# Mixture-of-experts kernel on one core: results of experts 0 to 6 added to x by one-hot products in the next expert, in place of indirect DMAs that add in device memory

## The reference

```python
def moe_swiglu(h, w_router, w_gate, w_up, w_down):
    logits = (hf @ w_router).astype(jnp.float32)
    top_val, top_idx = lax.top_k(logits, TOP_K)          # TOP_K = 2 of 8
    gates = jax.nn.softmax(top_val, axis=-1)
    ...
    def run_block(args):
        tok, gate, e = args
        y = swiglu(hf[tok], w_gate[e], w_up[e], w_down[e])   # 1024 -> 3584 -> 1024
        return y * gate[:, None].astype(y.dtype)
    ...
    out = jnp.zeros((N, D), h.dtype).at[buf_tok].add(y.reshape(cap, D).astype(h.dtype))

x = x + moe_swiglu(h, ...)
return rmsnorm(x, final_norm)
```

## Time and profile before

| what | value |
|---|---|
| median of 3 runs (lowest, highest) | 1356.46 us (1355.63, 1356.54) |
| the profiled execution's own time | 1358.75 us |
| its span, first to last instruction | 1357.0 us |
| PE busy | 1314.3 us (97%) |
| PE weight loads busy | 941.6 us (69%) |
| DVE / ACT / POOL busy | 427.5 / 305.1 / 80.2 us |
| read from device memory | 438.70 MB |
| expert 0 begins on PE | about 504 us |

### The profile page before, as it was taken

One profiled execution on the slowest core, in us unless ns is written; L12 is line 12 of the kernel. 1 busy time (PEld: TensorE's weight loads), 2 busy tenths in 40 slices (PEclk: granted clock), 3 DMA queues, 4 the chain that ended last, 5 costly groups with the idle time before them and its releaser, 6 DMA issues.

```text
span 1357.0 us, 31023 instructions
## 1 busy us (share of the span) xinstructions
PE 1314.3 (97%) x13973; PEld 941.6 (69%) x13973; DVE 427.5 (32%) x719; ACT 305.1 (22%) x467; POOL 80.2 (6%) x76
## 2 busy tenths in 40 slices
PE   7999999999999999999999999999989999999985
PEld 7999999878888886665556666665546666665543
DVE  6987878965444560000000000000000000000002
ACT  5455455554444460000000000000000000000002
POOL 1511111010000000000000000000000000000000
PEclk9999999999999999999999999999999999999998
DMA  9644454357665578999999999999999999999993
GB/s 355 250 166 151 147 187 184 128 180 280 248 245 218 182 284 358 372 386 403 419 412 419 417 421 406 420 418 406 419 421 412 419 418 405 421 418 418 408 420 152
DMA packets 68425, 447.45 MB, mean 330 GB/s; under 512 B 7920, under 2 KB 10608, under 8 KB 16192
## 3 DMA queue, kind: packets, MB, share of 16 engines
q1 hardware_dynamic: 63456, 436.57, 80.1%
q0 software_dynamic: 4400, 8.30, 2.3%
q10 hardware_dynamic: 432, 0.54, 0.1%
HBM read 438.70 MB, written 6.68 MB: 328 GB/s over the span
## 4 chain that ended last, share of the span: by engine, by line
PE 89%; DMA 5%; SPq 4%; ACT 1%; DVE 1%; issue 1%; ACTq 0%; DVEq 0%
PE bank L1783 37%; PE bank L1802 14%; PE bank L444 10%; PE bank L446 10%; PE bank L445 10%; SPq L465 3%; DMA raw_late<-in_expert_units 2%; DMA w_raw<-in_expert_units 2%; PE bank L1730 2%; PE bank L1546 1%; PE bank L1528 1%; PE bank L1561 1%; PE bank L1762 1%; DMA qkT<-in_xT 1%; PE bank L1536 0%
## 5 line engine op out<-in xcount | busy, mean ns | idle before, releaser
L400 DVE TENSOR_TENSOR w_lo<-raw,w_hi 128x2048 fp32r<-128x2048 f32 x70 | 160.5, 2293 | 60.6 <-ACT w_hi L395 60.4
L395 ACT ACTIVATE w_hi<-raw 128x2048 fp32r<-128x2048 f32 x71 | 135.9, 1914 | 90.1 <-PE bank L446 84.1
L444 PE MATMUL bank<-w_hi,a_hi 128*128 128x256 f32 (+1 forms) x400 | 136.5, 341 | 1.0 <-DVE a_lo L1154 0.5
L446 PE MATMUL bank<-w_hi,a_lo 128*128 128x256 f32 (+1 forms) x400 | 133.9, 335 | 0.0
L445 PE MATMUL bank<-w_lo,a_hi 128*128 128x256 f32 (+1 forms) x400 | 133.9, 335 | 0.0
L1280 DVE TENSOR_TENSOR h<-sg,bank 128x384 f32<-128x384 f32 (+1 forms) x56 | 28.2, 504 | 301.8 <-PE bank L1802 163.1
L1286 DVE COPY hT_x<-bank 128x128 f32<-128x128 f32 x35 | 10.1, 290 | 352.3 <-ACT hT_x L842 352.3
L444 PE MATMUL bank<-a_hi,w_hi 128*128 128x256 f32 x384 | 112.4, 293 | 8.6 <-DVE w_lo L982 8.6
L446 PE MATMUL bank<-a_hi,w_lo 128*128 128x256 f32 x384 | 110.2, 287 | 0.0
L445 PE MATMUL bank<-a_lo,w_hi 128*128 128x256 f32 x384 | 110.2, 287 | 0.0
L842 ACT ACTIVATE hT_x<-bank 128x256 f32<-128x256 f32 x35 | 13.4, 383 | 420.1 <-PE bank L1730 420.1
(11 more groups left out here) (302 smaller groups left out, 1861.0 us busy)
## 6 DMA issues: line engine op xcount, KB each, us to landing
w_raw<-in_expert_units SPq DMA_DIRECT2D x86, 1024.0 KB, 28.1
raw<-in_units SPq DMA_DIRECT2D x71, 1024.0 KB, 4.9
raw<-in_expert_units SPq DMA_DIRECT2D x60, 1024.0 KB, 27.6
raw_more<-in_expert_units SPq DMA_DIRECT2D x45, 1024.0 KB, 27.4
raw_late<-in_expert_units SPq DMA_DIRECT2D x45, 1024.0 KB, 27.6
extra<-in_expert_units SPq DMA_DIRECT2D x30, 1024.0 KB, 26.9
a_raw<-in_expert_units SPq DMA_DIRECT2D x28, 1024.0 KB, 26.5
aside_raw<-in_expert_units SPq DMA_DIRECT2D x15, 1024.0 KB, 27.5
```

The costliest lines, as they stand in the source:

```text
L395: nc.scalar.activation(w_hi[:, u % SPLIT, :], where, ACT.Copy).then_inc(hi_ready, 1)
L400: nc.vector.tensor_tensor(w_lo[:, u % SPLIT, :], home(u)[0], w_hi[:, u % SPLIT, :].bitcast(F32), ALU.subtract).then_inc(lo_ready, 1)
L444: nc.tensor.matmul(bank, hi, w[0], start=start, stop=False)
L446: return nc.tensor.matmul(bank, lo, w[0], start=False, stop=stop)
```

## The change

It does four things.

1. The indirect DMAs that add `y_rows` to `sums` go for experts 0 to 6, with the read of `sums` (L620), the add of it (L1313) and six of the eight early stores of zeros. They stay only in the branch that is not taken.
2. ACT's `results` puts the scaled results of a token's slot side by side in one row of `y_rows` (64 rows of near tokens by 1024 columns, 32 rows of far ones): two instructions for bank 0 and, for a wide expert, four for bank 1, in place of one and one.
3. In expert i+1 PE makes four products of 128 tokens x 512 columns from `place` and `y_rows` (`place_results`), two for tokens 0 to 127 in block 0 and two for tokens 128 to 255 in block 1, into banks 0 and 1. DVE adds each to x (`add_results`). The first down unit waits for the four adds (`banks_free`).
4. `place` is now made for every expert: two transposes of `pick` in block 3 and ACT's copy. `pick_slots` moves from block 3 to 4, `slot_sums` and `slots_known` from block 4 to 5.

```diff
-            def scatter(i, parity, wide, total):
+            def scatter(i):
                 pool.wait_ge(y_scaled, i + 1)
...
             for i in range(1, E):
                 gather(i, i % 2, IS_WIDE[i])
-                total += 2 if IS_WIDE[i - 1] else 1
-                scatter(i - 1, (i - 1) % 2, IS_WIDE[i - 1], total)
-            pool.wait_ge(unit_used, U_MOE + LAST_IN_HN + 1)
-            pool.dma_start(hn[:, :, :], sums[0:SEQ, :].rearrange("(t p) d -> p t d", p=P)).then_inc(sums_back, 16)
-            pool.sem_inc(scatter_done, 1)
+            pool.wait_ge(x_added, 4)
+            pool.sem_inc(scatter_done, E)
...
-                    for table, at in ((hn_rows, EMPTY), (sums, 0), (sums, P), (sums, EMPTY)):
+                    for table, at in ((hn_rows, EMPTY), (sums, EMPTY)):
...
             def results(i, parity, wide):
                 act.wait_ge(unit_used, U_MOE + (i + 1) * UE)
                 act.wait_ge(spots_ready, i + 1)
-                if not isinstance(i, int) or i:
-                    act.wait_ge(scatter_done, i)
-                last = nc.scalar.activation(y_rows[:, 0:512], ps[0][:, :], ACT.Copy, scale=slot_gate[:, parity, 0:1])
+                for s in range(2):
+                    of = slice(s * NEAR, (s + 1) * NEAR)
+                    last = nc.scalar.activation(y_rows[0:NEAR, s * 512:(s + 1) * 512], ps[0][of, :], ACT.Copy,
+                                                scale=slot_gate[of, parity, 0:1])
                 if wide:
-                    last = nc.scalar.activation(y_rows[:, 512:768], ps[1][:, 0:256], ACT.Copy, scale=slot_gate[:, parity, 1:2])
+                    for s in range(4):
+                        of = slice(s * FAR, (s + 1) * FAR)
+                        last = nc.scalar.activation(y_rows[NEAR:WIDE, s * 256:(s + 1) * 256], ps[1][of, 0:256], ACT.Copy,
+                                                    scale=slot_gate[of, parity, 1:2])
...
-                    if last and (kind, b, half) == ("up", 2, 1):
-                        act.wait_ge(place_tr, 1)
+                    if isinstance(i, int) and (kind, b, half) == ("up", 3, 1):
+                        act.wait_ge(place_tr, i + 1)
                         nc.scalar.activation(place[:, :], ps[7][:, 0:SEQ], ACT.Copy).then_inc(place_ready, 1)
...
+            def add_results(i, t):
+
+                for n in range(2):
+                    dve.wait_ge(y_placed, 4 * i + 2 * t + n + 1)
+                    cols = x[:, t, n * 512:(n + 1) * 512]
+                    nc.vector.tensor_tensor(cols, cols, ps[n][:, :], ALU.add).then_inc(x_summed, 1)
...
+                    if i and (kind, b, half) == ("up", 0, 1):
+                        add_results(i - 1, 0)
+                    if i and (kind, b, half) == ("gate", 1, 1):
+                        add_results(i - 1, 1)
                     if i == E - 1:
-                        if (kind, b, half) == ("gate", 4, 0):
-                            dve.wait_ge(sums_back, 16)
-                            for t in range(TT):
-                                nc.vector.tensor_tensor(x[:, t, :], x[:, t, :], hn[:, t, :], ALU.add).then_inc(x_summed, 1)
                         return
-                    if (kind, b, half) == ("gate", 3, 0):
+                    if (kind, b, half) == ("gate", 4, 0):
                         pick_slots(i + 1, slice(i + 1, i + 2))
-                    if (kind, b, half) == ("up", 4, 0):
+                    if (kind, b, half) == ("up", 5, 0):
                         slots_known(i + 1, (i + 1) % 2, IS_WIDE[i + 1])
...
+            def banks_free(i):
+
+                if not isinstance(i, int):
+                    pe.wait_ge(y_scaled, i)
+                elif i:
+                    pe.wait_ge(x_summed, 4 * i)
+
+            def place_results(i, t):
+
+                pe.wait_ge(place_ready, i + 1)
+                pe.wait_ge(y_scaled, i + 1)
+                if t:
+                    pe.wait_ge(x_summed, 4 * i + 2)
+                slots = WIDE if IS_WIDE[i] else NEAR
+                for n in range(2):
+                    nc.tensor.matmul(ps[n][:, :], place[0:slots, t * P:(t + 1) * P], y_rows[0:slots, n * 512:(n + 1) * 512],
+                                     start=True, stop=True).then_inc(y_placed, 1)
...
                 for j, (kind, b, half) in enumerate(MOE_SEQ):
+                    if (kind, b, half) == ("up", 0, 1):
+                        place_results(i - 1, 0)
                     narrow_unit(i, j)
...
                     if b:
                         turn_hidden(i, b - 1, True)
                         after(b)
+                    elif isinstance(i, int) and i:
+                        place_results(i - 1, 0)
...
+                    if i and b == 1:
+                        place_results(i - 1, 1)
+                    if b == 3:
+                        pe.wait_ge(spots_ready, i + 1)
+                        for t in range(TT):
+                            first = 0 if i == E - 1 else NEAR
+                            turned = pick[:, t, :, :].rearrange("p a n -> p (a n)")[:, first:first + P]
+                            last = nc.tensor.transpose(ps[7][:, t * P:(t + 1) * P], turned.bitcast(F32), ident[:, :])
+                        last.then_inc(place_tr, 1)
...
-                    if i < E - 1 and b == 4:
+                    if i < E - 1 and b == 5:
```

More of the change, by code:

```diff
@@ L98 @@
     _free.append(_n)
-LAST_IN_HN = max(_n for _n in range(MAIN) if SLOT_OF[_n] == N_FIRST)
 AGAIN = 14
@@ L627, in _ @@
                     gather(i, 0, True)
-                    scatter(i, 0, True, 2 * (i - E + 1) + total)
+                    scatter(i)
                 pool.nop()
@@ L862, in expert @@
                         hidden_near(i, b - 1 if kind == "gate" else b + 1, wide)
-                    if last and (kind, b, half) == ("up", 2, 1):
-                        act.wait_ge(place_tr, 1)
+                    if isinstance(i, int) and (kind, b, half) == ("up", 3, 1):
+                        act.wait_ge(place_tr, i + 1)
                         nc.scalar.activation(place[:, :], ps[7][:, 0:SEQ], ACT.Copy).then_inc(place_ready, 1)
-                if not last:
+                if not isinstance(i, int):
+                    results_again(i)
+                elif not last:
                     results(i, parity, wide)
@@ L1239, in pick_slots @@
                     dve.wait_ge(row_sum_ready, i)
+                if isinstance(i, int) and i:
+                    dve.wait_ge(place_tr, i)
                 for t in range(TT):
@@ L1249, in slots_known @@
                 dve.wait_ge(row_sum_ready, i + 1)
-                if not isinstance(i, int) or i >= E:
+                if not isinstance(i, int):
                     dve.wait_ge(scatter_done, i)
                 elif i >= 2:
-                    dve.wait_ge(scatter_done, i - 1)
+                    dve.wait_ge(y_scaled, i - 1)
                 for part in range(2 if wide else 1):
@@ L1305, in after @@
                         slots_known(0, 0, IS_WIDE[0])
-                    if i == 0 and (kind, b, half) == ("gate", 4, 0):
+                    if i == 0 and (kind, b, half) == ("gate", 5, 0):
                         dve.wait_ge(overs_summed, 1)
                         nc.vector.tensor_scalar(over_i[:, :], ps[7][:, 0:1], 1.0, None, ALU.min).then_inc(routed, 1)
+                    if i and (kind, b, half) == ("up", 0, 1):
+                        add_results(i - 1, 0)
+                    if i and (kind, b, half) == ("gate", 1, 1):
+                        add_results(i - 1, 1)
                     if i == E - 1:
-                        if (kind, b, half) == ("gate", 4, 0):
-                            dve.wait_ge(sums_back, 16)
-                            for t in range(TT):
-                                nc.vector.tensor_tensor(x[:, t, :], x[:, t, :], hn[:, t, :], ALU.add).then_inc(x_summed, 1)
                         return
-                    if (kind, b, half) == ("gate", 3, 0):
+                    if (kind, b, half) == ("gate", 4, 0):
                         pick_slots(i + 1, slice(i + 1, i + 2))
-                    if (kind, b, half) == ("up", 4, 0):
+                    if (kind, b, half) == ("up", 5, 0):
                         slots_known(i + 1, (i + 1) % 2, IS_WIDE[i + 1])
@@ L1417, in _ @@
                 .then_inc(y_right_scaled, 1)
-            dve.wait_ge(x_summed, TT)
             for q, (n, t, bank) in enumerate(SCATTER):
@@ L1813, in begin @@
                     pe.wait_ge(hT_near_ready, i * N_EB + b + 1)
-                    if b == 0 and (not isinstance(i, int) or i):
-                        pe.wait_ge(y_scaled, i)
+                    if b == 0:
+                        banks_free(i)
                 if kind == "gate" and b == 0 and isinstance(i, int) and i == 0:
@@ L1896, in after @@
                         slot_sums(0, slice(0, 1), IS_WIDE[0])
-                    if i == 0 and b == 3:
-                        pe.wait_ge(spots_ready, 1)
```

(12 more changed lines are left out.)

26 lines of the change are left out of this document (15 added, 11 removed).

## The result

The changed kernel takes **1366.01 us** (median of 6 runs, 1365.22 to 1366.57) against 1356.35 for the kernel before (6 runs, 1355.63 to 1357.02): ratio 1.0072, 95% interval 1.0059 to 1.0085, so 9.7 us slower. The prediction was 1359.8 with a range to 1364.5. The kernel gets slower, as predicted, but the size is not as predicted: 2.4 us by the sum and 3.3 by the number, 9.7 as measured.

What follows compares the result with a forecast made beforehand. PE and the weight loads were taken to bound the kernel in turns. Adding 27.7 us to PE against 25.3 free ends 2.4 us later with PE alone pacing; scaled, 1359.8 us, range 1353.5 to 1364.5.

Steps and rivals of the forecast that it cites:

- The products, 3.75 us an expert: On PE in experts 1 to 7: four 512-column products at 3.44 us plus a 0.31 switch, 26.2 for seven.
- The transposes, 0.22 an expert: On PE: two added transposes of pick for each of experts 0 to 6, 0.11 each, 1.5 us in all.
- The loads stay ahead, and the relief is worth nothing: Weight loads land 10 to 18 us before last use; 16 us taken from the DMA engines counts as 0.
- One drain more for a narrow result: Narrow results' 64-row products, as their own tiling mode, might pay another switch at two experts, some 0.6 us over the sum.
- ACT and DVE, nothing on the path: At the results' hand-over: ACT's 3.1 us and DVE's 2.5 us an expert stay covered, so PE doesn't wait.
- rival 3: New wait at each hand-over from ACT or DVE, 0.5 to 1 us an expert: 1364 us, chance 0.15.
- Rival 2: Products cheaper by running beside neighbours, 20 to 25 us in all: 1354 us, chance 0.2.
- Rival 1: Loads still set the end, so bytes removed from the DMA show as time: some 1342 us, chance 0.12.
- What PE has free: 25.3 us: PE's waits for loads in experts 4, 5 and 7, 5.07 + 4.37 + 15.9, can absorb added work.
- On which scale: Profiled execution against the runs' median: 1361.2 or 1358.9 us; a third of the 2.3 us between taken, giving 1359.8.
- The gather ... cover 7 us: Gather for the next expert, a block later: some 11 us needed within 18.7, leaving 7 us cover, more in wide experts.
- the four rivals: The prediction's alternatives: loads set the end, cheaper products, hand-over waits, and adds in device memory staying (chance nil).

Runs made afterwards that it cites:

- e3: Changed kernel with every one-hot product of experts 0 to 6 made twice; 1391.46 us.
- e1: Changed kernel without the one-hot products and DVE's adds for experts 0 to 6, their results left out of x; 1343.04 us.
- e10: Kernel before, with pick also transposed and copied to place in experts 1 to 6, copies unused; 1357.81 us, one execution.
- e2: Changed kernel with POOL also making the former adds in device memory, with their waits, into a table nobody reads; 1365.95 us.
- e6: Changed kernel with POOL, in a wide expert, issuing the gather only after the far parts of block 5; 1361.30 us.
- e12: Kernel before, unedited, profiled a second time; 1355.69 us.
- e9: Kernel before, with only the slots' work (pick, slot sums, slot numbers, gather) a block later; 1356.20 us, one execution.

## Why the prediction was right in kind and short in size

**The products, 3.75 us an expert.** Measured 3.78 (81.01 - 77.23), and 3.44 for the four alone by e3, which leaves 0.34 for the switch where the prediction had 0.31. The nearest row, the 512-column unit, was the right one. Right.

**The transposes, 0.22 an expert.** 77.23 - 77.01 in e1 and e10. Right.

**The loads stay ahead, and the relief is worth nothing.** No wait for a landing from 600 to PE's last unit, and in the last 19 us before it the DMA engines are idle:

```profile
1330.00:1349.00 19.00, 19.00 (x172) 11.95 (x168) 1.43 (x4) 0.94 (x3) 0.00 (x0) 1.00 0.00 1
```

The last two units are made from 1345.2 on, so their loads were there 15 us or more before, at the upper end of the forecast's 10 to 18 or a little beyond; the loads into `hn` in 855:935 land 5.7 to 10.4 us after their issue, where it had "some 10 of the 26". e2 shows the 0. Right.

**One drain more for a narrow result.** The prediction took from the Trainium skill, "TensorEngine Tiling (Array Packing)", section Key Properties, that changing the tiling mode drains TensorE. By that rule the 64-row products of experts 2 and 5 would pay one switch more, about 0.3 us in each. The traces show none: expert 5 of e6, with 64-row products, is 4.00 over the 115.73 of a wide expert, and expert 1, with 96-row ones, is 4.00 over its 77.01. For the switch between 64 columns and the whole width they do show a price, the 0.34 above.

**ACT and DVE, nothing on the path.** The trace has no wait of PE for either at these places, and expert 4 is as long as expert 1. Right; rival 3 falls with it. Rival 2 falls by e3. Rival 1 falls with the changed profile, in which no wait for a landing is left; e1 shows that its 1342 was well placed as what the loads allow, 1343.04 with no product at all.

**"What PE has free: 25.3 us."** This is the step that failed. It was read from the earlier trace rows of one execution, as 5.07 + 4.37 + 15.9. In e12, the same program in another execution, it is: expert 4, 77.01 - 77.01 = 0; expert 5, 120.98 - 117.65 = 3.3; expert 7, 90.75 less what it takes without waits, 80.16 - 3.78 = 76.38, gives 14.4 (the same sum gives 15.8 for the first profile, where the prediction had 15.9). Together **17.7**. Then 27.7 - 17.7 = 10.0, and 1355.7 + 10.0 = 1365.7, where 1366.0 was measured.

Of the 7.6 us between 25.3 and 17.7, 2.6 are loads that ran slower in the profiled execution (720.13 - 717.57 for experts 1 to 7), and the other 5.0 are PE's own longer work: 1.9 each in experts 2 and 5 and 0.65 and 0.53 in experts 3 and 6. Most of it is the stalls beside the gathers, which e6 prices at 4.7 in the changed kernel, expert 0 included. That the new sum comes within 0.3 is luck in part. Against e12's lengths and 4.00 more, expert 2 of the changed kernel is 1.7 longer and experts 3 and 6 are 2.0 and 1.2 shorter, and the stretches ahead of expert 1 and behind the last unit are 1.1 and 0.6 longer than in e12. These differences were not looked into.

**"On which scale."** The prediction saw that the profiled execution was 2.3 us above the median, saw that slow loads would make the free time too large, and took a third of it. It should have taken all of it: a kernel that PE paces gets none of it back. That alone would have given 1361.2, still within the range; the stalls at the gathers, 4.7 us by e6, took the time out of it. They could not be read from that profile, since its far parts ran without a pause (one row of 128 weight loads in 3.43 us); a second execution would have shown it.

**"The gather ... cover 7 us."** The cover held, since no one waits for the gathered rows. But what a gather costs PE by being issued was set at nothing, and it is 1.7 us beside far parts for a pair and 0.45 for a single one. None of the four rivals has such a stall either. That it costs the kernel before nothing, since its waits for loads take it up, is argued from the times of e9, e10 and e12 (1355.7 to 1357.8); the late gather was not tried in that kernel.

Why the first profile has none of these stalls stays open. Its execution took 1358.75, and some executions of the kernel before, without a profile, took 1357.5 to 1359.0 too; but e10 took 1357.81 and has the stalls, so the time alone doesn't tell. How the gather holds up PE's instructions was not tried beyond moving it, nor whether it is POOL's instruction or the transfers' start that does it.

## What to carry to other kernels

Slack is a small difference between two large numbers, and it belongs to one execution: where a forecast spends nearly all of it, profile a second execution, and if the profiled one stands above the median, take the whole difference off the slack. A change that trades transfers for TensorE work pays only while TensorE has time left; once it sets the end, every product counts in full, so the first thing to buy is a cheaper product (one pass for a one-hot matrix, row halves side by side). And look at what stands beside a dense stream of short matmuls: here POOL's indirect transfers were better issued beside long ones.

## What the runs showed of the hardware

- In 11 of 12 profiles an indirect transfer issued by POOL goes with a slower issue on PE when PE is in a stream of 128-column products with a weight load each (far parts): from about 0.9 us after the start of POOL's instruction, pauses of 0.3 to 0.6 us, one for one transfer, three for two (about 0.45 and 1.7 us in all). Beside 512-column products (e6), no pause shows. The narrow experts, whose stream is of 256 and 512 columns, stay at 81.01 and 77.01 with two transfers each. Whether the short products or their use of a quarter of the columns matters was not tried.
- Other issue stalls, with weight loads 0.3 to 1.4 us late, fall elsewhere, most in far parts, as in expert 2 of the changed kernel, which takes 1.7 us more than expert 5. They stay at their instructions when the gather is moved (e6), their places differ otherwise from kernel to kernel, and no run here was made on them.
- Four 512-column fp32 products over all columns take 3.44 us, in the single-pass type 0.94 (an estimate, 3.44 - 2.50, if the switch costs the same). A pair of 64 rows each on the two row halves takes 0.78 us less than the 1.72 of two.
